# A sixth pair of depth blocks by seven block products in the first MLP product

## The reference

```python
D_MODEL = 2048; SEQ = 256; D_FF = 4 * D_MODEL
h = rms_norm(x, mlp_norm[l])
x = x + jnp.square(jax.nn.relu(h @ w_mlp_in[l])) @ w_mlp_out[l]
```

## Time and profile before

| | |
|---|---|
| median of 3 runs (lowest, highest) | 2205.86 us (2204.42, 2207.76) |
| the profiled execution: its time, its span | 2204.39 us, 2202.3 us |
| busy: PE, PEld, DVE, ACT, POOL | 99%, 82%, 74%, 49%, 4% |
| group 2 starts | 1632.7 us |
| one group with the second product behind it | some 87 us |

### The profile page before, as it was taken

One profiled execution on the slowest core, in us unless ns is written; L12 is line 12 of the kernel. 1 busy time (PEld: TensorE's weight loads), 2 busy tenths in 40 slices (PEclk: granted clock), 3 DMA queues, 4 the chain that ended last, 5 costly groups with the idle time before them and its releaser, 6 DMA issues.

```text
span 2202.3 us, 26688 instructions
## 1 busy us (share of the span) xinstructions
PE 2184.9 (99%) x10174; PEld 1802.3 (82%) x10174; DVE 1636.6 (74%) x2109; ACT 1081.8 (49%) x1385; POOL 85.7 (4%) x72
## 2 busy tenths in 40 slices
PE   8999999999999999999999999999999999999999
PEld 6887778878887878888888888888888888888887
DVE  7999777778787789655775555655688878878874
ACT  5545345444444555545464455445555545445452
POOL 0000000000000000000001100000100000000000
PEclk9999999999999999999999999999999999999999
DMA  9998587978797669635456454566556556456462
GB/s 373 378 346 304 189 284 260 353 278 335 260 336 253 203 245 360 234 121 187 158 185 215 155 183 138 182 192 188 184 200 229 192 172 229 157 205 213 169 215 92
DMA packets 140290, 504.01 MB, mean 229 GB/s; under 512 B 15713, under 2 KB 16513, under 8 KB 139393
## 3 DMA queue, kind: packets, MB, share of 16 engines
q1 hardware_dynamic: 139808, 502.09, 65.8%
q10 hardware_dynamic: 354, 0.22, 0.0%
HBM read 500.13 MB, written 2.11 MB: 228 GB/s over the span
## 4 chain that ended last, share of the span: by engine, by line
PE 92%; DMA 3%; DVE 3%; ACT 1%; issue 0%; POOL 0%; SPq 0%; DVEq 0%; ACTq 0%
PE ps L1290 68%; PE ps L1345 8%; PE ps L1300 7%; PE ps L1411 3%; PE ps L1359 2%; DMA raw<-in_ret_in 2%; DVE raw L2021 1%; DVE wlo L1953 1%; DMA arena<-in_ret_in 1%; PE ps L1512 0%; PE ps L1490 0%; PE ps L1489 0%; PE ps L1438 0%; DVE alo L1953 0%; PE ps L1334 0%
## 5 line engine op out<-in xcount | busy, mean ns | idle before, releaser
L1953 DVE TENSOR_TENSOR wlo<-raw,whi 128x1024 fp32r<-128x1024 f32 (+1 forms) x555 | 664.3, 1208 | 325.4 <-ACT whi L1594 322.8
L1594 ACT ACTIVATE whi<-raw 128x1024 fp32r<-128x1024 f32 (+1 forms) x555 | 571.0, 1040 | 530.8 <-PE ps L1290 378.5
L1290 PE MATMUL ps<-whi,ahi 128*128 128x512 f32 x1990 | 632.9, 397 | 1.9 <-DVE alo L2060 1.2
L1290 PE MATMUL ps<-whi,alo 128*128 128x512 f32 x1990 | 618.1, 390 | 0.0
L1290 PE MATMUL ps<-wlo,ahi 128*128 128x512 f32 x1990 | 617.6, 390 | 0.0
L1290 PEld LDWEIGHTS ps<-wlo,ahi 128*128 128x128 f32 x1990 | 373.6, 188 | 79.8
L1290 PEld LDWEIGHTS ps<-whi,alo 128*128 128x128 f32 x1990 | 373.6, 188 | 79.4
L1290 PEld LDWEIGHTS ps<-whi,ahi 128*128 128x128 f32 x1990 | 365.2, 188 | 75.5 <-issue 4.0
L2021 DVE SCALAR_TENSOR_TENSOR raw<-raw,arena 128x1024 f32<-128x1024 f32 x184 | 223.5, 1218 | 0.0
L1953 DVE TENSOR_TENSOR wlx<-raw,whx 128x1024 fp32r<-128x1024 f32 x56 | 70.0, 1291 | 19.4 <-ACT whx L1594 19.4
L1345 PE MATMUL ps<-whi,ahi 128*128 128x512 f32 x194 | 76.5, 394 | 0.0
(11 more groups left out here) (303 smaller groups left out, 2619.7 us busy)
## 6 DMA issues: line engine op xcount, KB each, us to landing
raw<-in_mlp SPq DMA_DIRECT2D x204, 512.0 KB, 4.2
raw<-in_ret_in SPq DMA_DIRECT2D x188, 512.0 KB, 5.2
raw<-in_ada_t SPq DMA_DIRECT2D x184, 512.0 KB, 5.1
raw<-in_in SPq DMA_DIRECT2D x80, 512.0 KB, 4.1
raw<-in_ret_out SPq DMA_DIRECT2D x64, 512.0 KB, 4.8
late<-in_mlp SPq DMA_DIRECT2D x52, 512.0 KB, 4.8
raw<-in_mla_in SPq DMA_DIRECT2D x48, 512.0 KB, 4.6
raw<-in_mla_out SPq DMA_DIRECT2D x32, 512.0 KB, 4.1
```

The lines of the kernel that those rows point to most:

```text
L1290: mm = e.matmul(acc_[:, :], (ahi, alo, ahi)[m][:, slot, kb, tb * P:(tb + 1) * P], parts[m][:, chunk(n)], start=begins, stop=False)
L1594: e.activation(high(i)[:, 0:ncol], raw_of(n)[:, 0:ncol], ACT.Copy).then_inc(*s_hi.up(i))
L1953: e.tensor_tensor(low(i)[:, 0:ncol], raw_of(n)[:, 0:ncol], high(i)[:, 0:ncol].bitcast(F32), ALU.subtract).then_inc(*s_lo.up(i))
```

## The change

Pair 2 becomes a fast pair too, so six of eight are. The order of the pairs is 2, 3, 4, 0, 5, 6, 7, 1: two runs of three fast pairs, each with a plain pair behind it. `shi` and `slo` get a sixth part, and for this five small tables (`sums`, `cols`, `gate_col`, `mod`, `mhalf`) move into the space that the late tiles share. The sixth kept input lies in the first 512 columns of `rawx`, so the first load of group 2 (`n == united`, which goes to `rawx`) waits until its rows are summed.

```diff
-PAIRS = (3, 0, 4, 5, 1, 6, 7, 2)
-FAST = {k2: k2 - 3 for k2 in range(3, 8)}
+PAIRS = (2, 3, 4, 0, 5, 6, 7, 1)
+FAST = {k2: k2 - 2 for k2 in range(2, 8)}
...
-        sums = sb("sums", [P, 2, 16, 6])
...
-        cols = sb("cols", [P, NCOL + -NCOL % 16])
...
-        gate_col = sb("gate_col", [P, 2, 16])
-        mod = sb("mod", [P, 2, 2, 16])
...
-        mhalf = sb("mhalf", [P, 64])
...
             dg = early.enter_context(nc.sbuf_tensor("dg", [P, 2, P], F32))
+            sums = early.enter_context(nc.sbuf_tensor("sums", [P, 2, 16, 6], F32))
+            cols = early.enter_context(nc.sbuf_tensor("cols", [P, NCOL + -NCOL % 16], F32))
+            gate_col = early.enter_context(nc.sbuf_tensor("gate_col", [P, 2, 16], F32))
+            mod = early.enter_context(nc.sbuf_tensor("mod", [P, 2, 2, 16], F32))
+            mhalf = early.enter_context(nc.sbuf_tensor("mhalf", [P, 64], F32))
...
-        kept = {k2: late[:, 4096 + i * 512:4608 + i * 512] for k2, i in FAST.items()}
+        kept = {k2: late[:, 4096 + i * 512:4608 + i * 512] if i < 5 else late[:, 2048:2560] for k2, i in FAST.items()}
...
+                if n == united:
+                    w.wait_ge(*s_vec.on(("kept", "h3", 7)))
```

## The result

The changed kernel takes 2219.81 us (median of 4 runs, 2218.87 to 2222.16) where the kernel before takes 2205.70 beside it; the ratio is 1.0064, 95% interval 1.0052 to 1.0077. That is 14.1 us more, inside the range of 2214 to 2236; 21 us more were forecast. The profiled execution took 2218.87 us, its span is 2217.1 us. Its lines are numbered two higher from line 1216 on: 1290 is 1292, 1300 is 1302.

The account below looks back on a forecast made before the run. PE is busiest over the span, but DVE is nearly full in the fast-pair stretch. DVE's lateness of 17.4 us plus 3.4 for the clock gives 20.8, so 2225.2 profiled, 2227 us against the median; range 2214 to 2236 us.

Parts of the forecast that it names:

- rival 3: Groups 2 to 7: PE's waits come and `whx` matmuls also get faster by address, 2226.7 - 4.8 = 2222 us; chance 25%.
- the clock: Behind pair 7's waits: PE's clock falls, 1.7 us each; two falls taken, 3.4 us, bounds none and 10.2 us.
- the addresses: `whx` matmuls behind pair 7: moved tables put `whx` at a multiple of 256; bounds 0 and -4.8 us, 0 taken.
- DVE's chain: Group start to pair 7's low part: DVE late, +2.45 us in each of groups 3 to 7, +5.1 in group 2.
- The waits of PE: Group 3's fast pairs: PE waits 0.5 us at pair 6, then 0.7 (high part) and 1.9 (low part) at pair 7.
- Costed at nothing: Sixth input sum in groups 0 and 1, SP's wait before the first `rawx` load, and the DMAs: no cost to PE.
- Rival 4: Behind the waits: the clock falls in every group, 2205.9 + 17.4 + 10.2 = 2233.5 us; chance 12%.
- Rival 1: At pair 7: DVE's lead covers the added work, no wait, 2201.7 us, or 2194 with the address effect; chance 7%.

Follow-up runs that it names:

- both edits: Changed kernel with PE making low-part products last, and ACT's high and DVE's low parts of a fast pair's piece written in halves: 2193.35 us, ratio 0.9949.
- second comparison: The changed kernel run again unaltered, beside other kernels on one chip: 2216.57 us, ratio 1.0057 to the kernel before.
- padded kernel: Changed kernel with 64 bytes of padding behind `stat`: 2220.68 us, ratio 1.0072 to the kernel before.
- low parts last: Changed kernel with PE making the products with high weight parts first and those with low parts last in fast products: 2210.56 us, ratio 1.0023.
- four and two: Changed kernel with pair order 2, 3, 4, 5, 0, 6, 7, 1, a run of four fast pairs and one of two: 2217.65 us, ratio 1.0062.

## Why the prediction was right, and where its sizes were off

The direction, the cause and the range held: slower, because DVE's work for pair 7 is too late. The forecast itself was 7 us too high: 2219.8 lies below its 2223 to 2230 and closest to rival 3, at 2222, which had a chance of 25%. Two terms of the sum made the difference, the clock (3.4 us) and the addresses (4.8 us).

**DVE's chain: right, to 0.05 us.** The 3.7, 11.2, 20.1, 27.6 and 33.35 us of the prediction were 3.7, 11.2, 20.1, 27.6 and 33.3. In group 2 the low part of pair 7 was due at T + 35.9; the chain has it at 1667.90 + 2.30, 35.9 behind 1634.3. Pair 7's third matmul was to come 2.45 us later in group 3 than before; it comes at 1758.92, T + 33.34, 2.4 us later. That DVE's sum is the cause, and not something that comes at the same time, is shown from three sides: another order with the same sum gave the same length to 0.05 us, 0.8 us less of DVE's waiting three times a group gave back 2.4 us a group, and wanting the low part 1.36 us of matmuls later gave back 1.36. The kernels with five fast pairs have no wait of PE from group 2 on, and the one with six and both edits has 0.8 us.

**The waits of PE** were split as said, pair 7's last and longest. The prediction counted delays of a start, so they are compared with starts: pair 6's was 0.87 us (1750.32 to 1751.42, less 0.23) and not 0.5, since PE came to it earlier on matmuls of 0.2267 us. Pair 7's for the high part was 0.73 where 0.7 was said, and for the low part 1.75 and not 1.9: the first matmul behind the wait for the high part took 0.34 us to the next start and not 0.23, and filled a part of it.

**Costed at nothing: right.** SP's wait, the sixth input sum and the DMAs left no wait of PE.

**The clock: mis-sized.** "I take two falls, 3.4 us": there was none in either profile of the changed kernel. Falls do come at such waits: one each in the padded kernel and in the one with low parts last, two with four and two, each starting within 1 us of the end of a wait of 1.6 to 1.9 us, and none from group 2 on in the kernels without such waits. Most such waits had no fall behind them. The windows show the padded kernel's (PEclk third from the end of a row):

```profile
2022.00:2026.00 4.00, 2.05 (x7) 1.38 (x8) 3.66 (x2) 4.00 (x5) 0.00 (x0) 0.95 0.08 15
2026.00:2030.00 4.00, 4.00 (x12) 3.15 (x12) 4.00 (x5) 2.89 (x5) 0.00 (x0) 0.62 0.92 339
```

That is group 6, 91.0 us long where group 5 is 89.0; 0.3 of the 2.0 us group 6 has without a fall too, which leaves the 1.7 of the prediction. With low parts last, the fall, also behind pair 7, cost 1.1 us by the same count (88.7 against 87.33). The two with four and two cost nothing that the length of a group shows, the one in group 2 (91.4 against 91.3) nor the one in group 6 (88.99 against 88.95): both lie ahead of the wait for pair 7, in which the lost time disappears, as the prediction had it for an early fall. Rival 4 (a fall in every group) didn't come.

**The addresses: mis-sized, rival 3.** "Bounds 0 and -4.8; I take 0" should have been the other bound. With 17.4 - 4.8 = 12.6 us and no falls the sum is 2218.3; the changed kernel measured 2219.8, 14.1 us above the kernel before, and in the second comparison 12.2 us above it. The traces show the size: from pair 7's third matmul to the next group it was 55.98 us in group 3 before and is 55.34, 0.64 us less, where 0.8 was the bound. Where PE sets the time the effect is larger, 8.7 us.

**Rival 1** (the lead covers it) had the wrong lead but a right price: where the waits are removed, 2193.35 us was measured, and its 2194 was 2201.7 less the address effect. The Trainium skill's rule on it (Perfetto Trace Analysis, Identifying the Most-Contended Engine) would have gone for PE by its share of the span; the trace agrees on the span (weight loads 81%, DVE 75%) and disagrees for the stretch in which the sixth pair fell: in the 33.3 us from T of group 3 DVE was busy 29.96 us and the weight loads 24.25. The same page's Optimization Strategy says that in some kernels the most-contended engine changes over time, and this trace agrees with that: DVE without a gap but for 0.8 us waits from T + 1.8 on, and slack behind.

## What to carry to other kernels

Price an edit on the engine that is full in that stretch, not over the span: the sixth pair takes 0.7 us of work from PE in a group, and on the same layout it made the group 3.1 us longer, because DVE, busy 75% of the span, was full for just those 30 us. If operations are too late by a fixed time, look at what is wanted first and at what a producer waits for needlessly: an order of matmuls and a split of one activation (and of the subtraction behind it) gave back 23 us without less work. And a change of layout is a change by itself: try it alone. It was worth 8.7 us in the kernel before, and in the comparison of the two kernels it covered a part of what the sixth pair cost.

## What the runs showed of the hardware

Where the tiles lie in a partition had a price, and much of it goes with the distance between the tile that matmuls stream and the tile from which their stationary operand is loaded. With `whx` a multiple of 256 bytes from `ahi`, matmuls of 512 columns came 0.2267 us apart; 64 bytes below such a multiple 0.2333, 128 bytes off 0.2327 in the mean (5.57 us for 24 in the chain above), 64 bytes above 0.2295. In the kernel before, `whx` and `ahi` were the odd pair, and fast products of `whi` with `shi`, also an odd 64 apart, came 0.229 apart. The Trainium skill (SBUF — State Buffer, Who interferes with whom) gives TensorE two independent read ports, one for the moving operand and one for the weight load, and says that PE never waits on anyone; the time from start to start of the same instructions without and with 64 bytes of padding, 0.2333 and 0.2267, doesn't fit a plain reading of that, and here the measurement decides. The distance of two tiles is not the whole of it: `whx`, `shi` and `slo` are multiples of 256 bytes apart in every kernel, and yet in the kernel before a fast matmul of `whx` with `shi` took 0.2328 us to the start of the next, which loads from `slo` (mean of 58), and one of `whx` with `slo`, in front of one that loads from `shi`, 0.2270; with 64 bytes above it was 0.2307 and 0.2301. What else counts, each tile's own address or the traffic of the other engines, was not separated: only the late tiles were shifted.
